# First gated layer: the two transposes that spread the norm's factor, moved behind eight matmuls of the third panel

## The reference

```python
def rms_norm_2(x, g):
    xf = x.astype(jnp.float32)
    y = xf * lax.rsqrt(jnp.mean(xf * xf, axis=-1, keepdims=True) + NORM_EPS)
    return (y * g.astype(jnp.float32)).astype(x.dtype)

def swiglu(h, w_in, w_out):
    gu = h @ w_in
    gate, up = jnp.split(gu, 2, axis=-1)
    return (jax.nn.silu(gate) * up) @ w_out
...
        x = x + FFN_RES_SCALE * swiglu(rms_norm_2(x, ffn_norm[i, 0]), ffn_w_in[i, 0], ffn_w_out[i, 0])
```

## Time and profile before

| | us |
|---|---|
| median of 3 executions | 1616.55 (1616.12 to 1616.74) |
| the profiled execution | 1616.26 |
| its span in the profile | 1614.5 |
| PE busy | 1600.7 (99%) |
| DVE busy | 1277.4 (79%) |
| ACT busy | 964.4 (60%) |
| POOL busy | 88.6 (5%) |

### The profile page before, as it was taken

The page is one execution under the profiler, slowest core; times in us unless marked ns, Lnnn a source line. Parts: engine busy times, 40 slices in busy tenths (PEclk is TensorE's granted clock), DMA queues, the critical chain, the costliest instruction groups (busy, mean ns, idle before and its releaser), DMA issues.

```text
span 1614.5 us, 25621 instructions
## 1 busy us (share of the span) xinstructions
PE 1600.7 (99%) x9237; PEld 1348.6 (84%) x9237; DVE 1277.4 (79%) x1884; ACT 964.4 (60%) x1466; POOL 88.6 (5%) x117
## 2 busy tenths in 40 slices
PE   9999999999999999999999999999999999999998
PEld 7888888887778888888888888888888888788886
DVE  5987898875969889788884757888878787778887
ACT  7743655555866555666554636665566655866654
POOL 1441000011000000100000000000010000100000
PEclk9999999999999999999999999999999999999999
DMA  8322554573125545555466445554655546245553
GB/s 333 137 101 106 208 182 187 212 289 131 53 81 207 182 182 209 195 199 190 180 244 245 179 157 182 184 195 172 231 186 186 202 182 218 96 154 185 191 193 111
DMA packets 41522, 292.83 MB, mean 181 GB/s; under 512 B 4928, under 2 KB 4960, under 8 KB 7008
## 3 DMA queue, kind: packets, MB, share of 16 engines
q1 hardware_dynamic: 40032, 283.05, 48.1%
q0 software_dynamic: 1264, 8.41, 1.5%
q10 hardware_dynamic: 144, 0.26, 0.0%
HBM read 290.65 MB, written 1.05 MB: 181 GB/s over the span
## 4 chain that ended last, share of the span: by engine, by line
PE 95%; ACT 2%; DVE 2%; issue 1%; POOL 0%; POOLq 0%; DVEq 0%; ACTq 0%
PE ps L785 27%; PE ps L791 14%; PE ps L749 11%; PE ps L751 11%; PE ps L760 11%; PE ps L846 3%; PE ps L850 3%; PE ps L847 3%; PE ps L871 1%; PE ps L1275 1%; PE ps L1077 1%; PE ps L1078 1%; PE ps L1086 1%; PE ps L1597 1%; PE ps L1583 1%
## 5 line engine op out<-in xcount | busy, mean ns | idle before, releaser
L2485 DVE TENSOR_TENSOR w_lo<-raw,w_hi 128x1024 fp32r<-128x1024 f32 x460 | 547.5, 1215 | 102.8 <-ACT w_hi L1769 102.2
L1769 ACT ACTIVATE w_hi<-raw 128x1024 fp32r<-128x1024 f32 x459 | 462.4, 1038 | 131.3 <-PE ps L760 111.8
L785 PE MATMUL ps<-h_both,w_hi 128*128 128x512 f32 x1920 | 461.5, 391 | 0.4 <-DVE h_both L2565 0.3
L785 PEld LDWEIGHTS ps<-h_both,w_hi 128*128 128x128 f32 x1920 | 352.1, 188 | 69.8 <-issue 1.7
L791 PEld LDWEIGHTS ps<-h_both,w_lo 128*128 128x128 f32 x1920 | 247.7, 191 | 10.4
L791 PE MATMUL ps<-h_both,w_lo 128*128 128x256 f32 x1920 | 250.9, 283 | 0.0
L1906 ACT ACTIVATE tm<-ps 128x512 f32<-128x512 f32 x120 | 71.7, 598 | 180.6 <-PE ps L791 180.3
L749 PE MATMUL ps<-w_hi,hid_hi 128*128 128x512 f32 x436 | 170.5, 391 | 0.0
L751 PE MATMUL ps<-w_hi,hid_lo 128*128 128x512 f32 x436 | 169.8, 389 | 0.0
L2642 DVE TENSOR_TENSOR tm<-ps,tm 128x512 f32<-128x512 f32 x120 | 82.9, 691 | 93.8 <-ACT tm L1906 93.3
L749 PE MATMUL ps<-w_hi,h_both 128*128 128x512 f32 x368 | 146.7, 399 | 0.5 <-DVE h_both L2565 0.5
(11 more groups left out here) (423 smaller groups left out, 1989.9 us busy)
## 6 DMA issues: line engine op xcount, KB each, us to landing
raw<-in_stream SPq DMA_DIRECT2D x264, 1024.0 KB, 4.8
ns_w<-in_ns_w POOLq DMA_DIRECT2D x1, 4096.0 KB, 17.4
ln_rows<-in_ln_rows POOLq DMA_DIRECT2D x2, 1024.0 KB, 10.2
row_const<-in_const_rest SPq DMA_DIRECT2D x1, 1076.0 KB, 19.3
raw<-in_second_halves SPq DMA_DIRECT2D x2, 512.0 KB, 6.8
x_sb<-in_x SPq DMA_DIRECT2D x1, 1024.0 KB, 9.1
row_const<-in_fin_rows POOLq DMA_DIRECT2D x2, 512.0 KB, 7.4
out<-x_row SPq DMA_DIRECT2D x3, 256.0 KB, 2.5
```

What stands on the lines that cost most here:

```text
L785: pe.matmul(bank[c], w_hi[:, slot, cols], h_both[:, :, k, :], start=(k == 0), stop=False)
L1769: act.activation(w_hi[:, static % 2, part], raw[:, r % RING, part], ACT.Copy).then_inc(hi_ready, 1)
L2485: dve.tensor_tensor(w_lo[:, static % 2, part], raw[:, r % RING, part], w_hi[:, static % 2, part].bitcast(F32), ALU.subtract).then_inc(lo_r ...
```

## The change

In layer `ffn00` alone, panel 2 is taken out of PE's loop and `rms_rows` is called inside it, behind the first eight of its matmuls. The other gated layers keep `rms_rows` ahead of panel 2.

```diff
-            def multiply_turned(q, b, bs, halves=(0, 1), fresh=None):
+            def multiply_turned(q, b, bs, halves=(0, 1), fresh=None, within=None):
...
                             pe.matmul(bank[c], w_hi[:, slot, cols], h_both[:, :, k, :], start=(k == 0), stop=False)
+                    if s == 0 and within:
+                        within()
                 for s in halves:
                     pe.wait_ge(lo_ready, 2 * panel + s + 1)
...
-                if f_count == 1:
+                if after_final(layer):
+                    multiply_turned(up, 2, 2, within=rms_rows)
+                    first = 3
+                elif f_count == 1:
                     rms_rows()
                 turns, rest = steps(first, up.blocks)
```

## The result

The changed kernel takes 1617.75 us (median of 22 executions), the kernel before 1616.19 (22 executions beside it): 1.56 us more, ratio 1.0014 with a 95% interval of 1.0007 to 1.0020. The change costs about 0.1%. The profiled execution took 1617.72 us, its span is 1615.9.

What follows compares the result with a forecast made beforehand. PE's one long queue of matmuls, 95% of the chain that ended last, was taken as the bound. The later transposes add 1.32 us to the 1616.55 us median: 1617.9 us, range 1616.9 to 1619.2.

Steps and rivals of the forecast that it cites:

- The two waits: In `ffn00`, PE loses 0.64 us to `rstd` ahead of panel 2 and 0.36 us to panel 1's sum at panel 3.
- a second wait: Ahead of panel 3, PE waits 0.22 us for DVE's sum of panel 1, which hangs on the transposes too.
- The rigid chain: From transposes through ACT and DVE to panel 3, no step has slack, so all behind ACT's copy moves 1.32 us later.
- The sum: Panel 3's delay of 1.32 us stays on PE's queue and so on the program's end: 1616.55 + 1.32 = 1617.9 us.
- Rival (c), the clock: The pause ahead of panel 3 takes PE's clock down, costing 1.7 us more, 1619.6 us; chance 0.04.
- (a): The chain behind the transposes moves rigidly, panel 3 begins at about 669.2, time 1617.9 us; chance 0.84.
- Loop and code (d): Straight code behind the loop's branch and moved loops stall PE on code loading, some 2 us more, 1619.9; chance 0.05.

Runs made afterwards that it cites:

- peel_only: Kernel before with panel 2 taken out of PE's loop, transposes still ahead of it: +0.11 us against the kernel before, ratio 1.0002.
- before_both_early: Kernel before, transposes ahead of panel 2, with ACT's and DVE's split of panel 3's first half and ACT's table load moved earlier: -0.43 us against it.
- both_early: Changed kernel with ACT's and DVE's split of panel 3's first half and ACT's table load moved earlier: -1.05 us against the kernel before.
- split_early: Changed kernel with ACT and DVE splitting panel 3's first half ahead of the step that waits for the transposes: +0.12 us against the kernel before.
- after_again: The changed kernel once more, no edit: median 1617.85 us, +1.45 us against the kernel before.
- behind_16: Changed kernel with the transposes behind all sixteen w_hi matmuls of panel 2 instead of eight: +4.40 us against the kernel before.

## Why the prediction was right

**The two waits.** The step that decided was to name a second wait, of 0.22 us at panel 3, which the profile of before calls "issue". The order gave its name (the sum of panel 1). The profile after confirms it, as it puts the pause of 2.03 us down to that sum, and peel_only does so for the old place of the transposes (0.20, with DVE's sum named). before_both_early settles that the loop has no part in it: the loop stands there as in the kernel before, only the chain is shorter, and panel 3 comes 5.67 behind panel 2 instead of 5.90.

**The rigid chain.** Forecast: transposes at 663.05, copy at 663.46, sum's end at 669.05, panel 3 at 669.20. Measured, less the 0.11: 663.05, 663.47, 669.06 (668.49 + 0.68 - 0.11) and 669.20. Eight traces with the transposes at four places have a distance of 6.15 to 6.20, as nothing in the chain is touched, and each edit of the chain shortens it by what its links say.

**The sum.** +1.32 forecast, 1.56 and 1.45 measured in medians. The term is met in the traces: panel 3's place differs by 1.32, the last matmul's by 1.33. The rest of the medians fits the executions that lie 1.2 us or more above them: without these nine the medians are 1617.55 and 1617.59, 1.36 and 1.20 above those of the kernel before (its one such execution left out as well). As this takes executions from one end only, it doesn't show that they make up all of the 0.1 to 0.2 us. That the time itself, 1617.9 against 1617.75, came out so close is in part luck: I added the 1.32 to the median of three executions, which is 0.36 above that of all 22 (1616.55 and 1616.19), the change cost 0.24 more than I said, and the two misses nearly cancel.

**What I had wrong.** Rival (c), the clock, stood at a chance of 0.04, on the reading that 4 us of nothing at the end of the program leave the granted clock at 1.00. It is no case instead of (a) but one beside it: the one of them that was profiled loses 1.54 us by it (estimate in (c): 1.7), and by their times up to a fifth of the executions, which lie 1.2 to 2.4 us above the median, do the like. The row at the program's end was true, but it ends at 1612, and the one behind it, which I also had, says the opposite:

```profile
1612.00:1614.00 2.00, 0.00 (x0) 0.67 0.60 208
```

PE still does nothing there, and in finer steps the granted clock is 0.68 from 1612.5 to 1613 and 0.50 behind it, some 4.7 us after PE's last matmul ended (1607.95). In the thirteen traces of this case that fall comes at very different distances from the end of the last matmul, from 2.0 us (both_early: matmul's end 1607.32, clock 0.80 from 1609.0 to 1609.5, then 0.50) to 5.3 us (split_early). So one execution that stood for 4 us at 1.00 was no evidence against a fall after a pause of 2. The two falls in mid-program fit in between: in after_again the clock falls near 670.9, 3.4 us after PE stopped, and in behind_16 near 671.2, 4.1 us after; both times PE had already begun panel 3, which is why the pause itself reads 1.00. The Trainium skill (TensorE: Matmul & The Clock Gate, "Why this matters for your kernels") warns of long idle gaps in mid-kernel. The traces agree: half the clock behind the pause of 3.86 us, and in one of two executions already behind one of 2.03 us.

**Loop and code (d).** peel_only excludes it (panel 4 at -0.04, median +0.11); and in the changed kernel, too, PE is busy for all 85 us from 680 to 765.

## What to carry to other kernels

Ahead of moving a step back to spare its engine a wait, follow what hangs on the step until it comes back to the same engine, and compare the length of that way with the engine's own work in between: here the way back took 6.2 us, against 6.0 of PE's own work ahead of panel 3 before the change (before_both_early) and 4.0 after it (both_early), so that the delay of the step came back whole as a wait. First shorten the way back, above all by work that doesn't need the step and that fits into idle time ahead of it (a table load into 1.30 us, a split into 2.2), then move the step. Behind a link taken out the next one shows, so reckon with the second longest way and not with the link's duration.

## What the runs showed of the hardware

A pause of TensorE of 2.0 us was followed by a stretch at a granted clock of 0.50 in one of two profiled executions of the same program, and one of 3.9 us was so in the one profiled; panel 3 took 1.54 and 1.55 us longer than the 5.72 of the change. The clock was still 1.00 during the pause and fell 3.4 and 4.1 us after PE had stopped, when it was at work again; behind the program's last matmul, with PE idle, it fell after 2.0 to 5.3 us. So the place to look for the cost of a pause is the work behind it. Filling the pause of 3.9 us with matmuls that nobody needs made the kernel faster (+2.96 against +4.40); filling the one of 2.0 us hardly moved the median (+1.40 against +1.45).

In the program's first microseconds the column of the granted clock doesn't show the slow pace: it reads 1.00 for the whole window from 0 to 5, although six junk matmuls take 0.46 us each there and later ones 0.27.

Apart from this, single executions of several kernels, the one before among them (1 of 29, 1 of 33 and 1 of 29), are some 4 to 7 us longer than their median, at a mean clock of 0.994 to 0.997; none of them was profiled, and where in the program they lose it stays open.
